# Two transformer blocks on one core: a re-ordered instruction schedule, and fused high-weight matmuls of 512 columns in both feed-forward blocks

## The chip, the core and the metric

The kernel runs on one core of a Trainium2 chip. The metric is device time in microseconds, from the first to the last instruction of one execution plus the launch and end around it. The engines named below are TensorE (PE in the profile; its weight loads are PEld), VectorE (DVE), ScalarE (ACT), GpSimd (POOL) and SyncE (SP), which issues the transfers.

## The reference

Input `x` has 256 tokens of 1024 features, float32. The reference is two blocks in a row, cut here to what matters:

```python
# block 1
h = rms_norm(x); proj = h @ w_in                 # 8 projections
o_sb  = stick_breaking_attention(sb_q, sb_k, sb_v)     # 8 heads of 64
log_a = log_sigmoid(g_low @ w_gate_up + b) / 16
o_gla = silu(g_out) * rms_norm(gated_linear_attention(g_q, g_k, g_v, log_a))  # 4 heads
x = x + (sigmoid(gate_sb) * (o_sb @ w_proj_sb) + sigmoid(gate_gla) * (o_gla @ w_proj_gla)) @ w_out
x = rms_norm(x + square(relu(rms_norm(x) @ w_ff1)) @ w_ff2)            # 4096 hidden
# block 2
q, k, v, ... = rms_norm(x) @ w_in_2
kc, vc = gelu(blocks(k_c) @ w1) @ w2             # compressed keys and values
nsa  = sum over compressed, selected, window attention (8 heads, 2 groups), gated
conv = silu(layer_norm(depthwise_conv_31(a * sigmoid(ag))))
mem  = cross attention to 256 memory tokens
h = x + merge(nsa, conv, mem) @ w_out_2
out = h + (silu(hn @ w_gate) * (hn @ w_up)) @ w_down                    # 2816 hidden
```

## The kernel before, in words

**Precision.** Every large product is made from float32 data split in two parts for TensorE's fp32r input: hi is the value rounded to fp32r, lo the rest. `mm3` issues three matmuls into one accumulator: hi·hi, hi·lo, lo·hi (L562 to L564).

**Weight chunks.** All weights stream through a ring of three slots (`RING = 3`) as 143 chunks of 1 MB (128 partitions x 2048). SyncE loads chunk n into `raw` when the lo part of chunk n-3 is made; ScalarE casts it to `whi` (`split_hi`, L1115) once TensorE is done with chunk n-3; VectorE makes `wlo = raw - whi` (`split_lo`, L1638); TensorE takes the chunk when `wlo` is there. The order of the chunks is the list at the top of the kernel, and each engine's program is written out in that order, with each chunk's evacuation and side work at fixed places in it. Each engine runs its own program strictly in order.

**Chunk kinds.** A 256-wide projection chunk is 48 matmuls of 256 columns. A contraction chunk (`into_residual`) is 24 matmuls of 512 columns. A compression chunk (`wk0, wk1, wv0, wv1`, function `compress`) is 16 matmuls of 256 columns. Results of projections alternate between two PSUM banks; a bank must be evacuated (`drained`) before the next but one chunk uses it (`free_unit`).

**Block 1.** Chunk 0 is `low`. From chunk 9 on, stick-breaking attention (n = 9 to 18) and gated linear attention (GLA) run between the chunks. GLA has 8 units u, one every second chunk (n = 9 + 2u): `gla_sums` (two float32 matmuls of 512 columns, L714), ScalarE's exponential (L1240), GpSimd's factors (`gla_factors`: 14 products at L505 and one at L508 or L510), then one chunk later `gla_scores` (L722) and VectorE's mask and reduction (`gla_mask`, L1749 to L1756). `gla_values` follows every fourth chunk from n = 13. The chunks 19 to 26 are sigmoid gates, whose evacuation on ScalarE is Abs, Exp, Ln, then the cast of chunk n+3, then Exp.

**Feed-forward 1** is 16 pairs: `expand` (one `w_ff1` chunk, hidden features on partitions, both 128-feature halves in one PSUM bank) and `contract` (one `w_ff2` chunk). The order on TensorE is expand f+1, contract f. ScalarE relu (L1333) and square (L1335), VectorE square (L1848) and lo part (L1851). **Feed-forward 2** is 11 triples gate f+1, up f+1, down f; ScalarE takes tanh of the gate (L1596), VectorE multiplies.

**Between blocks** ("seams"), `block_norm` on VectorE and ScalarE normalises the residual, TensorE transposes it (`turn_normed`, L657), and ScalarE and VectorE make `hT_hi` (L1165) and `hT_lo` (L1708) before the next chunk can start. Event numbers: 0 before chunk `low`, 2 before feed-forward 1, 3 before block 2, 4 before feed-forward 2.

**Block 2.** s counts chunks from `kcvc`. The order before is kcvc, ca0, cg0, wk0, wk1, kk, q0, wv0, wv1, q1, vv, ca1, cg1, qm0, qm1, then gates. Key and query norms are seven "head sums" on TensorE (L883), fed by ScalarE squares (L1414). `hidden_turn` and small matmuls make compressed keys. VectorE computes 124 convolution taps (L1989) spread over s = 3 to 25 by `taps_by`. Attention units start at s = 8: scores at s, ScalarE exponentials (L1462) in the same s, transposes at s+2, values at s+3.

Of the kernel before, what the change touches and what calls it, by code (L numbers as in the profile page):

```python
# [13 lines left out]
P = 128  # L14
# [17 lines left out]
def two_block_kernel(  # L32
# [90 lines left out]
    ATT = [(k, a, g) for a in range(TT) for g in range(2) for k in "swc"] + [("m", a, 0) for a in range(TT)]  # L123
    ATT_AT = 8

    with ExitStack() as ctx:
# [17 lines left out]
        hT_hi = sb("hT_hi", [P, KT, T], F32R)  # L144
        hT_lo = sb("hT_lo", [P, KT, T], F32R)
# [38 lines left out]
        a_ls = xn[:, 0, :].rearrange("p (a n) -> p a n", a=TT)  # L184
# [9 lines left out]
        decay_sum = TMP[:, 0:1152].rearrange("p (l t) -> p l t", t=P)  # L194
        mask = TMP[:, 1152:2176].rearrange("p (l t) -> p l t", t=P)
# [7 lines left out]
        ACC_FLAT = [PS[:, 2 * a:2 * a + 2, :].rearrange("p b n -> p (b n)") for a in range(TT)]  # L203
        S_gla = TMP[:, 4352:4736].rearrange("p (i t) -> p i t", t=P)
# [45 lines left out]
        def gate_tile(name):  # L250
# [13 lines left out]
        hi_made, lo_made, chunk_used = sem("hi_made"), sem("lo_made"), sem("chunk_used")  # L264
        drained = [sem("drained0"), sem("drained1")]
# [14 lines left out]
        h1_relu, h1_sq, h1_hi, h1_lo = (sem(n) for n in ("h1_relu", "h1_sq", "h1_hi", "h1_lo"))  # L280
# [16 lines left out]
        taps, cv_mean, cv_mid, cv_sq, cv_var, cv_ln, cv_root, cv_exp, cv_y, cv_lin, cv_sig, cv_f, cv_hi, cv_lo = (  # L297
            sem(n) for n in ("taps", "cv_mean", "cv_mid", "cv_sq", "cv_var", "cv_ln", "cv_root", "cv_exp", "cv_y", "cv_lin",
# [132 lines left out]
        def _(pool):  # L431
# [30 lines left out]
            keep(decay_sum[:, 8, :], [[1, P]], 0, -1)  # L462

# [27 lines left out]
            def gla_factors(u):  # L491
# [8 lines left out]
                for l in range(LEVELS):  # L500
                    hf = 1 << l
                    e = E[:, l + 1 - a, :].rearrange("p (b s x) -> p b s x", s=2, x=hf)
                    d = QK[:, l, :].rearrange("p (b s x) -> p b s x", s=2, x=hf)
                    for s, m in ((0, k), (1, q)):
                        pool.tensor_tensor(d[:, :, s, :], e[:, :, s, :],  # L505
                                           m.rearrange("p (b s x) -> p b s x", s=2, x=hf)[:, :, s, :], ALU.mult)
# [1652 lines left out]
```

## Time and profile before

| | us |
|---|---|
| median of 3 runs | 997.95 |
| range of the runs | 995.75 to 1002.14 |
| the profiled execution, own time | 995.86 |
| its span, first to last instruction | 994.1 |

| engine | busy us | share of span |
|---|---|---|
| TensorE matmul | 952.6 | 96% |
| TensorE weight load | 873.4 | 88% |
| VectorE | 585.2 | 59% |
| ScalarE | 517.5 | 52% |
| GpSimd | 85.9 | 9% |

Mean granted TensorE clock of the span: 0.986. The transfers moved 155.37 MB, 156 GB/s on average. A matmul's row in the profile lasts longer than the distance to the next row, because matmuls are pipelined: 0.28 us for 256 columns where the next one starts 0.12 us later. So for TensorE the distance between starts counts, not the duration. The clock column PEclk is the share of full speed (2.4 GHz) that was granted; 0.5 is the other level, 1.2 GHz.

### The profile page before, as it was taken

The numbers are of one execution on the slowest core, as the hardware profiler recorded it, in microseconds if no ns is written. First come the engines' busy times: TensorE is split into PE (matmuls) and PEld (weight loads), VectorE is DVE, ScalarE is ACT, GpSimd is POOL, SyncE is SP. The second block draws the span as 40 slices with busy tenths as digits, with TensorE's granted clock in tenths as the row PEclk, the third lists the DMA queues.
The fourth block names the chain that finished last, engine by engine and source line by source line (L and its number), as shares of the span: only waits on it lengthen the run. The fifth ranks groups of instructions, "written<-read, shape, count | busy, mean of one in ns | idle before, by whom it ended". The sixth has DMA issues, their size and how long they took to land.

```text
span 994.1 us, 16151 instructions
## 1 busy us (share of the span) xinstructions
PE 952.6 (96%) x6700; PEld 873.4 (88%) x6700; DVE 585.2 (59%) x704; ACT 517.5 (52%) x738; POOL 85.9 (9%) x220
## 2 busy tenths in 40 slices
PE   7999999898999999999987889999999989999998
PEld 7998888888988999999887888888999879999997
DVE  5334455655766554554575996655685655555554
ACT  6445545465446444444367667776646453434332
POOL 8202332233010000000010000000000000000000
PEclk9899999999999999999999889999999999999999
DMA  8464332427555565555643554334334545555551
GB/s 265 149 198 133 108 105 85 129 92 238 170 172 170 173 197 184 208 169 176 204 151 104 170 169 128 107 107 128 128 128 170 169 127 176 197 177 183 196 170 43
DMA packets 121817, 155.37 MB, mean 156 GB/s; under 512 B 2649, under 2 KB 107201, under 8 KB 121762
## 3 DMA queue, kind: packets, MB, share of 16 engines
q1 hardware_dynamic: 120848, 151.57, 47.5%
q0 software_dynamic: 864, 2.98, 0.9%
q8 instruction: 40, 0.66, 0.3%
q14 instruction: 15, 0.12, 0.0%
q10 hardware_dynamic: 50, 0.04, 0.0%
HBM read 153.53 MB, written 1.05 MB: 155 GB/s over the span
## 4 chain that ended last, share of the span: by engine, by line
PE 84%; DVE 7%; ACT 5%; POOL 2%; issue 1%; DMA 0%; SPq 0%; ACTq 0%; DVEq 0%
PE PS L562 24%; PE PS L563 24%; PE PS L564 24%; DVE wlo L1638 3%; ACT whi L1115 2%; PE PS L722 1%; POOL TMP L505 1%; PE PS L974 1%; DVE AR L1989 1%; PE PS L944 1%; PE PS L714 1%; PE PS L925 1%; PE PS L681 1%; PE PS L670 1%; DMA res<-in_x_dram 0%
## 5 line engine op out<-in xcount | busy, mean ns | idle before, releaser
L1638 DVE TENSOR_TENSOR wlo<-raw,whi 128x2048 fp32r<-128x2048 f32 (+1 forms) x143 | 326.5, 2284 | 236.6 <-ACT whi L1115 236.5
L562 PE MATMUL PS<-hT_hi,whi 128*128 128x256 f32 x1224 | 353.3, 289 | 7.2 <-DVE hT_lo L1708 4.1
L563 PE MATMUL PS<-hT_lo,whi 128*128 128x256 f32 x1224 | 350.3, 286 | 0.0
L564 PE MATMUL PS<-hT_hi,wlo 128*128 128x256 f32 x1224 | 350.3, 286 | 0.0
L1115 ACT CAST whi<-raw 128x2048 fp32r<-128x2048 f32 (+1 forms) x143 | 270.6, 1893 | 117.8 <-PE PS L564 117.6
L562 PEld LDWEIGHTS PS<-hT_hi,whi 128*128 128x128 f32 x1224 | 239.2, 195 | 9.7 <-issue 4.5
L563 PEld LDWEIGHTS PS<-hT_lo,whi 128*128 128x128 f32 x1224 | 238.9, 195 | 1.0
L564 PEld LDWEIGHTS PS<-hT_hi,wlo 128*128 128x128 f32 x1224 | 238.8, 195 | 0.0
L562 PE MATMUL PS<-whi,aT_hi 128*128 128x512 f32 x216 | 84.3, 391 | 0.0
L563 PE MATMUL PS<-wlo,aT_hi 128*128 128x512 f32 x216 | 84.3, 390 | 0.0
L564 PE MATMUL PS<-whi,aT_lo 128*128 128x512 f32 x216 | 84.0, 389 | 0.0
L562 PE MATMUL PS<-whi,hT_hi 128*128 128x256 f32 (+1 forms) x240 | 76.5, 319 | 0.0
L563 PE MATMUL PS<-wlo,hT_hi 128*128 128x256 f32 (+1 forms) x240 | 74.7, 311 | 0.0
L564 PE MATMUL PS<-whi,hT_lo 128*128 128x256 f32 (+1 forms) x240 | 74.7, 311 | 0.0
L562 PE MATMUL PS<-oT_hi,whi 128*128 128x256 f32 x224 | 64.2, 287 | 5.3 <-ACT xn L1204 1.5
L563 PE MATMUL PS<-oT_lo,whi 128*128 128x256 f32 x224 | 63.4, 283 | 0.0
L564 PE MATMUL PS<-oT_hi,wlo 128*128 128x256 f32 x224 | 63.4, 283 | 0.0
L1989 DVE SCALAR_TENSOR_TENSOR AR<-AR,cw 128x256 f32<-128x256 f32 x120 | 49.4, 479 | 0.2
L562 PEld LDWEIGHTS PS<-oT_hi,whi 128*128 128x128 f32 x224 | 42.9, 192 | 6.5 <-issue 3.8
L563 PEld LDWEIGHTS PS<-wlo,hT_hi 128*128 128x128 f32 x240 | 45.7, 191 | 2.9 <-issue 0.5
L562 PEld LDWEIGHTS PS<-whi,hT_hi 128*128 128x128 f32 x240 | 45.7, 191 | 2.9 <-issue 0.5
L564 PEld LDWEIGHTS PS<-whi,aT_lo 128*128 128x128 f32 x216 | 40.6, 188 | 8.6
(336 smaller groups left out, 1145.5 us busy)
## 6 DMA issues: line engine op xcount, KB each, us to landing
raw<-in_w_in_dram SPq DMA_DIRECT2D x47, 1024.0 KB, 5.2
raw<-in_w_ff_dram SPq DMA_DIRECT2D x32, 1024.0 KB, 5.2
raw<-in_w_gate_dram SPq DMA_DIRECT2D x11, 1024.0 KB, 5.3
raw<-in_w_up_dram SPq DMA_DIRECT2D x11, 1024.0 KB, 5.3
raw<-in_w_down_dram SPq DMA_DIRECT2D x11, 1024.0 KB, 5.0
raw<-in_w_out_dram SPq DMA_DIRECT2D x8, 1024.0 KB, 4.9
raw<-in_w_proj_gla_dram SPq DMA_DIRECT2D x4, 1024.0 KB, 5.1
raw<-in_w_mem_kv_dram SPq DMA_DIRECT2D x4, 1024.0 KB, 5.1
```

The costliest lines, as they stand in the source:

```text
L505: pool.tensor_tensor(d[:, :, s, :], e[:, :, s, :], m.rearrange("p (b s x) -> p b s x", s=2, x=hf)[:, :, s, :], ALU.mult)
L562: pe.matmul(dst, a_hi, b_hi, start=start, stop=False, skip_group_check=True)
L563: pe.matmul(dst, a_hi, b_lo, start=False, stop=False, skip_group_check=True)
L564: return pe.matmul(dst, a_lo, b_hi, start=False, stop=stop, skip_group_check=True)
L670: pe.matmul(z[:, 0:256], kT_sb[r, h // 2, 0:P], qT_sb[r, h // 2, :], start=True, stop=False, skip_group_check=True)
L681: pe.matmul(z[:, 0:384], negtri[:, :], spv, start=False, stop=False, skip_group_check=True)
L714: mm = pe.matmul(PS[:, 6 + c, :], a_ls[:, a, h * P:(h + 1) * P], decay_sum[:, a + 4 * c:a + 4 * c + 4, :], start=True, stop=True)
L722: pe.matmul(PS[:, 6 + l // 4, (l % 4) * P:(l % 4) * P + P], QK[:, l, :], QK[:, l, :], start=True, stop=True)
L925: pe.matmul(PS[:, h % 2, h // 2 * L:(h // 2 + 1) * L], q, k, start=h < 2, stop=False, skip_group_check=True)
L1115: act.copy(whi[:, n % RING, 0:width], raw[:, n % RING, 0:width]).then_inc(hi_made, 1)
L1638: dve.tensor_tensor(wlo[:, n % RING, 0:width], raw[:, n % RING, 0:width], whi[:, n % RING, 0:width].bitcast(F32), ALU.subtract).then_inc(l ...
L1989: ins = dve.scalar_tensor_tensor(cacc[:, f, :], src, cw[:, f, k:k + 1], cacc[:, f, :], ALU.mult, ALU.add)
```

## The change

1. **Chunk order of block 2**: compression chunks alternate with full ones. Head sums, `hidden_turn` and the norms move with them; the two memory-key norms come later (e = 4, 5 instead of 0, 1), attention units of the first token tile run s, w, s, w, c, c. `taps_by` has 14 taps done by the end of s = 9 (43 before).
2. **GLA**: `gla_sums` uses fp32r: log decays split in hi and lo (`a_hi`, `a_lo`), the 0/1 matrix as `decay_r`: four fp32r matmuls in place of two float32 ones. For u = 5, 6, 7 ScalarE's exponential moves ahead of the cast, and VectorE makes three of the seven levels of factors.
3. **Start**: chunk `low` is used at 66 columns, chunk 1 is cast and split in two halves, and TensorE starts on the first.
4. **Seams**: the last quarter of transposes (`turn_last`) moves behind the first two k of the first chunk (events 2 and 4); a split is cut in half around the root of event 3; at event 4 one `split_lo` moves from ahead of `block_norm` to behind the turned tiles, and a table load moves behind them too.
5. **Feed-forward**: `hT_hi` and `hT_lo` become one tile `hT`, and `wide` replaces `expand` and `gate_or_up`: the high weights stream both parts in one 512-column matmul, the low weights the high part in one of 256. Each half of 128 features fills a bank; ScalarE copies the lo half out, VectorE adds the hi half. Feed-forward 1's loop is 2 x 6 steps and 3 written out (5 x 3 before).
6. A `cg` chunk's bank is freed by VectorE's minimum instead of by the product after the exponential.

```diff
+    key_chunk("kk", 0)
     compress_chunk(0, 0)
+    chunk("q0", cols(w_in_2, 0))
     compress_chunk(0, 1)
-    key_chunk("kk", 0)
-    chunk("q0", cols(w_in_2, 0))
+    key_chunk("vv", 1)
     compress_chunk(1, 0)
+    chunk("q1", cols(w_in_2, CW))
     compress_chunk(1, 1)
-    chunk("q1", cols(w_in_2, CW))
-    key_chunk("vv", 1)
...
-        FN_AT = [2, 4, 6, 7, 8, 10, 15]
+        FN_AT = [4, 6, 10, 11, 12, 14, 15]
...
-                return 62 * max(s - 2, 0) // 10 if s <= 12 else min(62 + 62 * (s - 12) // 13, 124)
+                return 2 * max(s - 2, 0) if s <= 9 else min(14 + 110 * (s - 9) // 16, 124)
...
                 for c in range(2):
-                    mm = pe.matmul(PS[:, 6 + c, :], a_ls[:, a, h * P:(h + 1) * P],
-                                   decay_sum[:, a + 4 * c:a + 4 * c + 4, :], start=True, stop=True)
+                    d = decay_r[:, a + 4 * c:a + 4 * c + 4, :]
+                    pe.matmul(PS[:, 6 + c, :], a_hi[a][:, h * P:(h + 1) * P], d, start=True, stop=False)
+                    mm = pe.matmul(PS[:, 6 + c, :], a_lo[a][:, h * P:(h + 1) * P], d, start=False, stop=True)
...
             for n in range(at["projs0"]):
                 name = list(at)[n]
                 evac(name)
+                if n in (19, 21, 23):
+                    gla_exp((n - 9) // 2)
                 split_hi(n + RING)
...
+                if n in (19, 21, 23):
+                    dve.wait_ge(gf_exp, (n - 9) // 2 + 1)
+                    for l in range(LOW_LEVELS, LEVELS):
+                        ins = gla_factor(dve, (n - 9) // 2, l)
+                    ins.then_inc(gf_up, 1)
...
+            def wide(n, bank, it=0, event=None):
                 take(n, it)
                 w_hi, w_lo = parts(n, CW)
                 for c in range(2):
                     for k in range(KT):
                         if c == 0:
+                            if event is not None and k == 2:
+                                turn_last(event)
                             turned(event, k)
-                        mm = mm3(PS[:, 4 + j, c * T:(c + 1) * T], w_hi[:, k, c * P:(c + 1) * P],
-                                 w_lo[:, k, c * P:(c + 1) * P], hT_hi[:, k, :], hT_lo[:, k, :], k == 0, k == KT - 1)
+                        f = slice(c * P, (c + 1) * P)
+                        pe.matmul(PS[:, bank + c, :], w_hi[:, k, f], hT[:, k, :, :].rearrange("p w t -> p (w t)"),
+                                  start=k == 0, stop=False, skip_group_check=True)
+                        mm = pe.matmul(PS[:, bank + c, 0:T], w_lo[:, k, f], hT_hi[:, k, :], start=False, stop=k == KT - 1,
+                                       skip_group_check=True)
...
             def relu_square(f, it=0):
...
+                act.copy(relu[:, j, :].rearrange("p (c t) -> p c t", c=2), two_banks(4 + 2 * (f % 2))[1]).then_inc(h1_b, 1)
+                act.wait_ge(h1_sq, f + 1 + 3 * it)
+                act.copy(aT_hi[:, j].rearrange("p a t -> p (a t)"), sq[:, j, :]).then_inc(h1_hi, 1)
...
+                dve.wait_ge(h1_b, f + 1 + 3 * it)
+                dve.tensor_tensor(s, two_banks(4 + 2 * (f % 2))[0], s, ALU.add).then_inc(h1_sum, 1)
+                dve.wait_ge(h1_sum, f + 1 + 3 * it)
+                dve.scalar_tensor_tensor(sq[:, j, :], relu[:, j, :], 0.0, relu[:, j, :], ALU.max, ALU.mult).then_inc(h1_sq, 1)
...
+                pe.wait_ge(s_gate, f + 1 + 2 * it)
+                wide(FFN2 + 2 + 3 * f, 4, it)
+                pe.wait_ge(s_up, f + 1 + 2 * it)
+                wide(FFN2 + 3 + 3 * f, 6, it)
                 down(FFN2 + 4 + 3 * f, f, j, it)
...
             block_norm(3, res, x3_of)
-            split_lo(after_ffn1 + 2)
+            split_lo_half(after_ffn1 + 2, 0)
             token_root(5)
             normed(5, [res[:, a, :] for a in range(TT)], [xn[:, a, :] for a in range(TT)], width=512)
+            split_lo_half(after_ffn1 + 2, 1)
...
-            for c in range(3):
+            for c in range(2):
                 split_lo(FFN2 - 1 + c)
             block_norm(4, xn, scaled_in_place(4))
             turned_lo(4, hT_hi, hT_lo, G_FFN)
+            split_lo(FFN2 + 1)
             split_lo(FFN2 + 2)
```

## Rows read from the trace of the kernel before

**Rows 1.** The page, parts 1, 4 and 5: busy, the chain's engines, the taps
```profile
PE 952.6 (96%) x6700; PEld 873.4 (88%) x6700; DVE 585.2 (59%) x704; ACT 517.5 (52%) x738; POOL 85.9 (9%) x220
...
PE 84%; DVE 7%; ACT 5%; POOL 2%; issue 1%; DMA 0%; SPq 0%; ACTq 0%; DVEq 0%
...
L1989 DVE SCALAR_TENSOR_TENSOR AR<-AR,cw 128x256 f32<-128x256 f32 x120 | 49.4, 479 | 0.2
```

**Rows 2.** A stretch: length; PE, PEld, DVE, ACT, POOL busy; clock; DMA; GB/s
```profile
514.00:593.00 79.00, 67.20 (x492) 63.35 (x493) 62.18 (x115) 49.13 (x89) 0.00 (x0) 0.89 0.53 160
```

**Rows 3.** Timeline, TensorE, feed-forward 1: start, duration, engine, line, instruction
```profile
399.93 0.39 PE L563 MATMUL PS<-wlo,aT_hi 128*128 128x512 f32 x1
...
402.20 0.39 PE L564 MATMUL PS<-whi,aT_lo 128*128 128x512 f32 x1
...
402.42 0.28 PE L562 MATMUL PS<-hT_hi,whi 128*128 128x256 f32 x1
...
407.10 0.28 PE L562 MATMUL PS<-hT_hi,whi 128*128 128x256 f32 x1
```

**Rows 4.** One line (L1333): durations in ns, first and last start
```profile
L1333 ACT ACTIVATE relu<-PS x16: 597/598/598, 324.1 to 486.9; 128x512 f32<-128x512 f32 x16
```

**Rows 5.** The same of L1596, the tanh of feed-forward 2
```profile
L1596 ACT ACTIVATE relu<-PS x11: 597/598/598, 815.7 to 980.1; 128x512 f32<-128x512 f32 x11
```

**Rows 6.** Groups, 345 to 485 us: busy us, mean ns, idle before
```profile
L1638 DVE TENSOR_TENSOR wlo<-raw,whi 128x2048 fp32r<-128x2048 f32 x26 | 59.6, 2292 | 39.7 <-ACT whi L1115 39.7
...
L1115 ACT CAST whi<-raw 128x2048 fp32r<-128x2048 f32 x25 | 47.6, 1902 | 31.2 <-PE PS L564 31.2
```

**Rows 7.** Timeline, TensorE: the sums of GLA unit 3, and the next
```profile
141.07 1.98 PE L714 MATMUL PS<-TMP,xn 128*128 128x512 f32 x4
142.89 0.27 PE L747 MATMUL PS<-ident,AR 128*128 128x128 f32 x1
```

**Rows 8.** Waits of TensorE: us in total, times, longest
```profile
PE PS L722 <- POOL TMP L510: 5.1, 2, 2.6
...
PE PS L722 <- POOL TMP L508: 1.7, 1, 1.7
```

**Rows 9.** Timeline, ScalarE: the exponential of GLA unit 5
```profile
183.23 1.00 ACT L1240 ACTIVATE TMP<-PS 128x1024 f32<-128x1024 f32 x1
```

**Rows 10.** Timeline, GpSimd: the factors of unit 5
```profile
184.31 4.73 POOL L505 TENSOR_TENSOR TMP<-TMP,AR 128x64 f32<-128x64 f32 x14 [14.93 <-ACT TMP L1240]
```

**Rows 11.** Timeline, VectorE: the reduction of unit 7
```profile
231.01 1.99 DVE L1756 TENSOR_REDUCE TMP<-TMP 128x128 f32<-128x1024 f32 x1
```

**Rows 12.** Timeline, TensorE: the values that need it
```profile
234.10 0.60 PE L739 MATMUL PS<-AR,TMP 128*128 128x256 f32 x2
```

**Rows 13.** Timeline, GpSimd and TensorE: unit 0's last factor and its scores
```profile
87.01 0.46 POOL L508 TENSOR_TENSOR TMP<-TMP,AR 128x128 f32<-128x128 f32 x1
...
87.53 1.71 PE L722 MATMUL PS<-TMP 128*128 128x128 f32 x13
```

**Rows 14.** Timeline, TensorE: start of chunk 1
```profile
18.32 0.38 PE L562 MATMUL PS<-hT_hi,whi 128*128 128x256 f32 x1 [2.01 <-DVE wlo L1638]
```

**Rows 15.** Timeline, TensorE, block 2: where it waited, chunks 2 to 11
```profile
538.48 0.30 PE L856 MATMUL PS<-whi,aT_hi 128*66 128x256 f32 x1 [1.76 <-DVE aT_hi L2045]
...
545.08 1.13 PE L883 MATMUL PS<-xn,negone 128*128 128x512 f32 x2 [2.66 <-ACT xn L1414]
547.31 0.55 PE L562 MATMUL PS<-hT_hi,whi 128*128 128x256 f32 x1 [1.11 <-DVE AR L1878]
...
573.17 0.63 PE L883 MATMUL PS<-TMP,negtri 128*128 128x30 f32 x2 [4.88 <-ACT TMP L1414]
```

**Rows 16.** Timeline, VectorE and ScalarE, seam before feed-forward 2
```profile
791.89 2.29 DVE L1638 TENSOR_TENSOR wlo<-raw,whi 128x2048 fp32r<-128x2048 f32 x1 [3.15 <-ACT whi L1115]
...
800.42 1.28 ACT L1095 ACT_TABLE_LOAD   x1
```

**Rows 17.** Timeline, TensorE: transposes at the same seam
```profile
803.51 0.66 PE L657 MATMUL PS<-ident,xn 128*128 128x128 f32 x4 [2.42 <-DVE hT_lo L1708]
```

More of the change, by code:

```diff
@@ L499, in gla_factors @@
                 q, k = gqT[:, h, tok], gkT[:, h, tok]
[L500 to L506, printed above, removed]
+                for l in range(LOW_LEVELS if u in LATE_UNITS else LEVELS):
+                    gla_factor(pool, u, l)
                 if a == 0:
@@ L583, in feature_major @@
                 n, u = at[name], unit_of[name]
-                take(n)
+                if n == 1:
+                    pe.wait_ge(lo_half, 1)
+                else:
+                    take(n)
                 w_hi, w_lo = parts(n, width)
+                m = LOW if name == "low" else P
                 for f in range(width // P):
@@ L646, in turn_normed @@
                         pe.wait_ge(xn_made, done)
-                    for q in range(4 if a else first):
+                    for q in range(4 if event in (0, 3) else 3):
                         if a == 1 and q == 2:
@@ L827, in _, with step1 @@
                 pe.wait_ge(drained[b], (units_before_ffn1 - b + 1) // 2)
-            expand(FFN1, 0, event=2)
-            with pe.Fori(0, (F1 - 1) // 3) as it:
-                for j in range(3):
-                    expand(FFN1 + 1 + 2 * j, (j + 1) % 3, it)
-                    contract(FFN1 + 2 + 2 * j, j, j, it)
+            wide(FFN1, 4, event=2)
+            def step1(f, it=0):
+                wide(FFN1 + 1 + 2 * f, 4 + 2 * ((f + 1) % 2), it)
+                contract(FFN1 + 2 + 2 * f, f, f % 3, it)
+            with pe.Fori(0, 2) as it:
+                for f in range(6):
+                    step1(f, 2 * it)
+            for f in range(12, F1 - 1):
+                step1(f)
             contract(after_ffn1 - 1, F1 - 1, 0, last=True)
@@ L1058, in _ @@
                 pe.wait_ge(drained[b], (units - b + 1) // 2)
-            def gate_or_up(n, bank, it=0, event=None):
-                take(n, it)
-                w_hi, w_lo = parts(n, CW)
-                for c in range(2):
-                    for k in range(KT):
-                        if c == 0:
-                            turned(event, k)
-                        mm = mm3(PS[:, bank, c * T:(c + 1) * T], w_hi[:, k, c * P:(c + 1) * P],
-                                 w_lo[:, k, c * P:(c + 1) * P], hT_hi[:, k, :], hT_lo[:, k, :], k == 0, k == KT - 1)
-                mm.then_inc(chunk_used, 1)
             def down(n, f, j, it=0, last=False):
@@ L1313, in _ @@
                     turned_hi(1, oT_hi, G_MEM)
-            junk_hT = [w[:, 0:4, :].rearrange("p f t -> p (f t)") for w in (hT_hi, hT_lo)]
+            junk_hT = [hT[:, 2 * i:2 * i + 2, :, :].rearrange("p f w t -> p (f w t)") for i in range(2)]
             block_norm(2, xn, junk_hT)
```

388 lines of the change are left out of this document (228 added, 160 removed).

## The prediction, made before the changed kernel ran

> **What bounds the kernel now.** I read the page's busy times and its chain first: TensorE is busy 96% of the span and holds 84% of the chain [rows 1]. Then the stretches: in the first eleven chunks of block 2 it is busy 67.2 of 79 us at clock 0.89 [rows 2]. Then the waits of TensorE and the timelines around them [rows 8, 14, 15, 17]. So there are two kinds of stretch. In the loops only fewer or shorter matmuls help. In the GLA part, the start of block 2 and the seams TensorE waits for VectorE, ScalarE or GpSimd, and there the order counts.
>
> What one matmul costs is read from start-to-start distances. From 399.93 to 402.20 lie 10 matmuls of 512 columns: 0.227 us each. From 402.42 to 407.10 lie 39 of 256 columns: 0.120 us each [rows 3]. At 2.4 GHz the columns alone take 0.213 and 0.107, so each instruction carries about 13 ns that do not grow with its columns. The feed-forward loops run at exactly this pace: the reads of the 16 expands span 162.8 us [rows 4], and one expand (48 x 0.120 = 5.8) plus 14 pairs (5.76 + 24 x 0.227 = 11.2) make 162.7. In feed-forward 2, 9 triples of 2 x 5.76 + 5.45 = 17.0 and one of 11.5 make 164.2, against 164.4 measured [rows 5]. No wait hides in either loop.
>
> **Part by part.**
>
> *Fused matmuls.* Three matmuls of 256 (0.360 us) become one of 512 and one of 256 (0.347): 13 ns less per group. There are 16 groups in a chunk and 16 + 22 = 38 chunks, so 608 groups: **7.9 us**. Columns streamed do not change, 12288 per chunk. The Trainium skill ("TensorE: Matmul & The Clock Gate", section "Wait — 56ns, not 53.3ns?") gives a fixed cost of about 2.5 ns per warm matmul. By it the fusion would be worth 608 x 2.5 ns = 1.5 us, an estimate from that page; the two distances of rows 3 disagree with it. Bounds of the term from rows: 0 (if the 13 ns go with every 256 columns, which the 0.227 speaks against) to 7.9.
>
> The new passes are hidden. In feed-forward 1 ScalarE now waits, between its two reads, for VectorE's add and square, and the casts of two chunks are queued behind it. From the end of an expand: copy 0.6, two VectorE passes of 512 elements (a 2048-element pass takes 2.29, so 0.6 to 0.7 each), ScalarE 0.6, cast 1.9, VectorE's split 2.3 [rows 4, 6]: 6.8, about 7 with handovers. TensorE needs that chunk after one contract and one expand, 5.45 + 5.55 = 11.0 us. Slack 4 us. In feed-forward 2 the gate and up banks are single, but each is refilled only 11 us after it was filled, and its copy and add come first in the queues: also hidden. Cost 0.
>
> *GLA sums.* Two float32 matmuls take 1.82 us [rows 7]; four fp32r ones would take 4 x 0.227 = 0.91. Eight units: 7.3. At unit 0, GpSimd ends at 87.47 and TensorE arrives at 87.53 [rows 13]: nothing is left there, and GpSimd's start follows the attention mask, not the sums. So 0.7 comes back as a wait. **6.6 us**. The gate's extra copy and subtraction lie in the first 35 us, where both engines wait for TensorE.
>
> *GLA units 5 to 7.* TensorE waits 5.1 + 1.7 = 6.8 us for GpSimd [rows 8]. ScalarE's exponential starts at 183.23 [rows 9] after a cast (1.9) and a gate exponential (0.6); moved ahead of both it starts about 2.3 earlier. GpSimd's 14 products take 4.73 [rows 10]; it keeps 8, which is 2.0 less. Together 4.3, more than any single wait (2.6), so all three go, and VectorE's six small products run beside. What is late next: VectorE's reduction of unit 7 ends at 233.00 [rows 11], and the values that need it started at 234.10 [rows 12], slack 1.1. The reduction is behind chunk 24's split, whose timing is set by the end of chunk 24, while TensorE now arrives 2.6 earlier: 1.5 comes back. Net **5.3 us**. Ends: 3 (the same at unit 5) and 6.8.
>
> *Start.* Chunk 1 waits 2.01 us for its split [rows 14]. With halves, cast and split before the first matmul shrink by half of 1.9 and 2.3, 2.1 us; VectorE is also held by the turned tiles, so **1.7 us**; ends 0 and 2.0. The 66-column `low` shortens work that nobody waits for: 0.
>
> *Block 2's order.* The four waits are 1.8, 2.7, 1.1 and 4.9: 10.4 us [rows 15]. They come where two compression chunks follow each other: TensorE is through one in 16 x 0.120 = 1.9 us, ScalarE and VectorE need 1.9 + 2.3 per chunk plus norms and taps. In the new order a full chunk (5.8 us) lies between them; VectorE has 29 fewer taps by the end of s = 9 (120 of them take 49.4 us [rows 1], so about 12 us less; these come back at s = 10 to 25, beside chunks of 5.8 us and more); and the `cg0` bank is freed before the split instead of behind it. Laying the queues out with these durations leaves waits of 0.5 us before the head sum of kk, 1.8 before that of q0 (ScalarE copies the keys twice first) and 0.8 and 1.2 before the second and third attention scores: 4.3. Gain 6.1. The clock 0.89 over 79 us is 8.7 us of full-speed time [rows 2]; about 1.5 of it fell into waits. I keep one stretch at 1.2 GHz behind the seam and one later, 3.4 in all: gain 3.8. The two memory-key norms arrive in chunks 12 to 14, where ScalarE is the tightest; laid out, 1 us. **9 us**; ends 3 (waits only move) and 15.
>
> *Seams.* Event 3: half a split (1.15) leaves ScalarE's and VectorE's path: 0.9. Event 4: the split at 791.89 holds VectorE until 794.18, and the first token tile of the last contraction is complete half a chunk (2.7 us) before TensorE ends it, so VectorE could have begun earlier; of the 2.3 us I take 1.4 (ends 0 and 2.3); the 1.28 us table load stands ahead of the turned tiles [rows 16], for which TensorE waits 2.4 [rows 17]: 1.3. `turn_last` makes the last quarter late by about 0.4 at events 2 and 4. **2.8 us**; ends 0.5 and 4.
>
> **Sum.** 7.9 + 6.6 + 5.3 + 1.7 + 9 + 2.8 = 33.3. The profiled execution's own time was 995.9, so 962.6. It lies 2.1 us under the median of the runs, 997.95, so the median after should be near **965**.
>
> **The rivals.**
> 1. *The waits of block 2 only change place* (chance 0.20). For it: ScalarE is the queue behind most of them, and its work per chunk stays. Against: VectorE, 62.2 of 79 us busy [rows 2], loses 12 us. Then 3 instead of 9, the clock low as before, and unit 5 adds a wait: 965 + 6 + 2 = 973.
> 2. *The fusion gives nothing* (0.05), the 13 ns being tied to data, not to instructions: 965 + 7.9 = 973. The page "TensorE: Matmul & The Clock Gate" of the Trainium skill, section as above, points towards this case.
> 3. *Block 2 stays at 2.4 GHz* throughout and its waits shrink further (0.12): 6 us more, 959.
> 4. *Slower than before* (0.02): the round trip ScalarE, VectorE, ScalarE ahead of the casts of feed-forward 1 becomes its bound. It decides once it exceeds 11.0 us from the expand's end; to eat 33 us and another 10 over 15 pairs it must be 2.9 us above, 14 us in place of 7. Nothing in rows 6 is near that: VectorE is idle 39.7 us of that stretch.
> 5. My forecast: 0.61, own range 958 to 972.
>
> **How the numbers follow.** Range 955 to 979: down to rival 3 with the start and seams at their good ends, up to rivals 1 and 2 with half of the lower bounds at once. One per cent is 10 us, about what a measurement of this kernel tells from no change. Slower by over 1% is rival 4 and unnamed mishaps, 0.02. Within 1% needs the terms at nearly all their lower ends (0 + 6.6 + 3 + 0 + 3 + 0.5 = 13), 0.05. Faster by over 1%: 0.93.
>
> **What would show it.** Right: in feed-forward 1 the reads of the 16 expands span 159.6 us (15 x 0.21 less), 512 and 256 columns at 0.227 and 0.120; no wait of the scores of units 5 to 7 for GpSimd, and one of about 1.5 us of unit 7's values for VectorE; TensorE's waits between chunks 2 and 11 of block 2 near 4; no table load between the seam's norm and its turned tiles. Wrong: a distance of 0.24 or more behind the fused matmul; TensorE waiting for `wlo` inside a loop; clock under 0.9 in the first chunks of block 2.

## The result, and the profile after

| | before | after |
|---|---|---|
| median of the runs | 997.03 us (4 runs) | 966.38 us (4 runs, 965.28 to 967.08) |
| profiled execution, own time | 995.9 | 966.8 |
| its span, mean granted clock | 994.1, 0.986 | 965.1, 0.993 |

The ratio is 0.9682, with a 95% interval of 0.9646 to 0.9719: 3.2% faster. The forecast was 965.

The page after, parts 1 and 4 [rows 1]: busy time, share and instructions of each engine, then the chain's engines:

```profile
PE 938.4 (97%) x6092; PEld 835.4 (87%) x6092; DVE 616.1 (64%) x764; ACT 529.0 (55%) x763; POOL 86.1 (9%) x203
...
PE 85%; ACT 6%; DVE 6%; issue 2%; POOL 1%; DMA 1%; SPq 0%; ACTq 0%; DVEq 0%; POOLq 0%
```

TensorE issues 608 matmuls fewer and bounds the kernel as before; VectorE has 31 us more work, and TensorE's only new waits for it are 0.5 us (L776) and 0.4 us (L1088). TensorE's waits in the list of waits (us in total, times, longest), where rows 8, 14, 15 and 17 stood:

```profile
PE PS L858 <- DVE hT L1774: 3.9, 4, 1.5
PE PS L585 <- DVE hT L1774: 3.2, 2, 1.8
PE PS L970 <- ACT TMP L1508: 2.0, 2, 1.1
...
PE PS L759 <- POOL TMP L533: 1.6, 2, 0.8
...
PE PS L938 <- ACT xn L1469: 1.5, 1, 1.5
...
PE PS L776 <- DVE TMP L1825: 0.5, 1, 0.5
PE PS L989 <- ACT TMP L1517: 0.4, 1, 0.4
...
PE PS L585 <- DVE wlo L1854: 0.2, 1, 0.2
```

**Where the 29.1 us between the two profiled executions went.** Set the two timelines side by side at the same event. The lead is how much earlier "after" reaches it; a minus sign marks a stage in which it lost time:

| up to | event, start before and after | lead | of it in this stage | forecast |
|---|---|---|---|---|
| sums of GLA unit 0 | 78.06, 74.73 | 3.3 | start 3.3 | 1.7 |
| values of unit 7 | 234.10, 220.71 | 13.4 | sums 5.5, units 5 to 7 4.6 | 6.6 and 5.3 |
| first read of feed-forward 1 | 324.08, 311.48 | 12.6 | seam -0.9, fusion 0.1 | -0.4 |
| last read of it | 486.9, 472.6 | 14.3 | fusion 1.7 | (7.9 in all) |
| first chunk of block 2 | 514.23, 499.10 | 15.1 | seam 0.8 | 0.9 |
| sums of the convolution | 733.10, 707.73 | 25.4 | block 2 10.2 | 9 |
| bank of `up` 0 read | 815.7, 788.6 | 27.1 | seam 1.6, fusion 0.2 | 2.3 |
| last of them | 980.1, 951.0 | 29.1 | fusion 1.9 | |

Every stage has the sign that was forecast; the fusion brought 3.9 in place of 7.9, the start twice its term.

**The clock.** Stretches (length, busy times, granted clock, DMA share, GB/s) around each stretch of TensorE at 1.2 GHz, first before, then after:

```profile
26.00:36.00 10.00, 10.00 (x48) 8.35 (x47) 3.58 (x3) 4.37 (x8) 6.42 (x18) 0.66 0.64 202
514.00:520.00 6.00, 5.77 (x35) 5.80 (x36) 4.64 (x8) 2.16 (x2) 0.00 (x0) 0.72 0.57 179
546.00:554.00 8.00, 6.89 (x35) 6.72 (x35) 7.93 (x13) 5.25 (x9) 0.00 (x0) 0.57 0.80 254
570.00:578.00 8.00, 4.83 (x28) 4.54 (x29) 7.90 (x19) 5.67 (x11) 0.00 (x0) 0.57 0.55 159
594.00:598.00 4.00, 4.00 (x23) 4.00 (x22) 3.64 (x6) 3.61 (x14) 0.00 (x0) 0.57 0.01 2
```

```profile
26.00:30.00 4.00, 4.00 (x21) 3.95 (x21) 2.59 (x3) 2.77 (x6) 3.73 (x5) 0.57 0.93 270
500.00:505.00 5.00, 5.00 (x31) 4.99 (x30) 3.59 (x5) 1.50 (x1) 0.00 (x0) 0.66 0.59 190
562.00:566.00 4.00, 4.00 (x24) 3.77 (x25) 3.20 (x10) 3.97 (x11) 0.00 (x0) 0.57 0.82 262
608.00:614.00 6.00, 6.00 (x31) 3.81 (x31) 3.10 (x13) 4.93 (x8) 0.00 (x0) 0.72 0.58 175
```

Length times (1 - clock), summed: 13.7 us lost before, 6.8 after. That is 6.9 of the 29.1, 1.7 of it at the start.

In each of the 14 profiles the loss is a multiple of 1.7 us, and the number of stretches differs from run to run of one kernel; that makes most of its scatter. So two numbers are given for each experiment below: its median, and the mean over its runs of span times granted clock ("full-speed time"), in which the stretches are left out. For the four runs of the changed kernel the second lies within 0.6 us of its mean; the third decimal of the clock alone is worth 0.5 us either way in one run. It has a weakness: a wait inside a stretch at 1.2 GHz is counted by half. The last column of the table below is the mean of span times (1 - clock). Before: 980.7 (15.3 us lost to the clock, 9 runs beside e1 to e4). After: 958.3 (6.3 lost). So of the 30.7 us between the medians 22.4 is less work and fewer waits, and some 8 to 9 is clock.

### The profile page after: what moved, and what is told of

The parts are those of the page before. It is cut to its first block, busy times and chain, and to the rows that moved or that the text cites. A ratio compares the mean times of both kernels' runs of the same rounds, so it can differ in the third digit from the quotient of the medians.

```text
span 965.1 us, 14962 instructions
## 1 busy us (share of the span) xinstructions
PE 938.4 (97%) x6092; PEld 835.4 (87%) x6092; DVE 616.1 (64%) x764; ACT 529.0 (55%) x763; POOL 86.1 (9%) x203
## 3 DMA queue, kind: packets, MB, share of 16 engines
HBM read 153.53 MB, written 1.05 MB: 160 GB/s over the span
## 4 chain that ended last, share of the span: by engine, by line
PE 85%; ACT 6%; DVE 6%; issue 2%; POOL 1%; DMA 1%; SPq 0%; ACTq 0%; DVEq 0%; POOLq 0%
PE PS L585 17%; PE PS L587 17%; PE PS L586 17%; PE PS L858 15%; PE PS L860 7%; ACT whi L1151 3%; DVE wlo L1695 2%; PE PS L759 1%; PE PS L1019 1%; PE PS L989 1%; PE PS L970 1%; POOL TMP L217 1%; DVE hT L1774 1%; PE PS L715 1%; DMA res<-in_x_dram 1%
## 5 line engine op out<-in xcount | busy, mean ns | idle before, releaser
L1695 DVE TENSOR_TENSOR wlo<-raw,whi 128x2048 fp32r<-128x2048 f32 x140 | 320.8, 2292 | 164.2 <-ACT whi L1151 163.9
L1151 ACT CAST whi<-raw 128x2048 fp32r<-128x2048 f32 x141 | 268.5, 1904 | 91.9 <-PE PS L587 91.8
L858 PE MATMUL PS<-hT,whi 128*128 128x512 f32 x608 | 216.4, 399 | 3.9 <-DVE hT L1774 3.9
L585 PE MATMUL PS<-hT,whi 128*128 128x256 f32 (+1 forms) x616 | 178.9, 290 | 3.4 <-DVE hT L1774 3.2
L586 PE MATMUL PS<-hT,whi 128*128 128x256 f32 (+1 forms) x616 | 175.9, 286 | 0.0
L587 PE MATMUL PS<-hT,wlo 128*128 128x256 f32 (+1 forms) x616 | 175.8, 285 | 0.0
L860 PE MATMUL PS<-hT,wlo 128*128 128x256 f32 x608 | 170.7, 281 | 0.0
L585 PEld LDWEIGHTS PS<-hT,whi 128*128 128x128 f32 (+1 forms) x616 | 119.7, 194 | 4.9 <-issue 3.6
L586 PEld LDWEIGHTS PS<-hT,whi 128*128 128x128 f32 (+1 forms) x616 | 119.6, 194 | 0.2
L587 PEld LDWEIGHTS PS<-hT,wlo 128*128 128x128 f32 (+1 forms) x616 | 119.3, 194 | 0.0
L860 PEld LDWEIGHTS PS<-hT,wlo 128*128 128x128 f32 x608 | 114.8, 189 | 0.9
L585 PE MATMUL PS<-whi,hT 128*128 128x256 f32 (+1 forms) x240 | 75.7, 316 | 0.0
L587 PE MATMUL PS<-whi,hT 128*128 128x256 f32 (+1 forms) x240 | 74.7, 311 | 0.0
```

Of the source, the lines that this page charges most:

```text
L585: pe.matmul(dst, a_hi, b_hi, start=start, stop=False, skip_group_check=True)
L586: pe.matmul(dst, a_hi, b_lo, start=False, stop=False, skip_group_check=True)
L587: return pe.matmul(dst, a_lo, b_hi, start=False, stop=stop, skip_group_check=True)
L858: pe.matmul(PS[:, bank + c, :], w_hi[:, k, f], hT[:, k, :, :].rearrange("p w t -> p (w t)"), start=k == 0, stop=False, skip_group_check=True)
L860: mm = pe.matmul(PS[:, bank + c, 0:T], w_lo[:, k, f], hT_hi[:, k, :], start=False, stop=k == KT - 1, skip_group_check=True)
L1151: act.copy(whi[:, n % RING, :], raw[:, n % RING, :]).then_inc(hi_made, 1)
```

## Experiments

Each is an edit of the changed kernel. The ratios are to the kernel before, on the same chip. e1 to e4, e5 to e8 and e9 to e12 ran on three chips, beside the kernel before (medians 997.43, 999.00 and 998.77; full-speed times 980.7, 981.0 and 980.7) but not beside the changed kernel. The intervals of all ratios but those of e8 and e9 overlap with that of after, so what is said below of differences of 1 to 5 us rests on the full-speed time and the traces. Single runs of e6 and e11 spread over 2 to 3 us in full-speed time, those of e9 over 1.4, of the others over 1.1 at most.

| | median | ratio (95%) | full-speed time | lost to the clock |
|---|---|---|---|---|
| after | 966.38 | 0.9682 (0.9646 to 0.9719) | 958.3 | 6.3 |
| e1 three matmuls of 256 | 969.54 | 0.9716 (0.9694 to 0.9738) | 962.5 | 5.4 |
| e2 low ones behind | 962.56 | 0.9656 (0.9635 to 0.9677) | 955.9 | 5.6 |
| e3 quarter turned ahead | 964.17 | 0.9666 (0.9644 to 0.9689) | 957.2 | 5.4 |
| e4 six products on GpSimd | 966.43 | 0.9685 (0.966 to 0.971) | 957.9 | 6.6 |
| e5 and reductions ahead | 964.16 | 0.9653 (0.9628 to 0.9677) | 955.5 | 7.1 |
| e6 old taps | 970.56 | 0.9721 (0.9692 to 0.9751) | 960.5 | 8.7 |
| e7 warm at the seam | 967.54 | 0.9685 (0.966 to 0.971) | 958.5 | 7.5 |
| e8 units 5 to 7 as before | 978.22 | 0.9794 (0.9769 to 0.982) | 964.8 | 11.7 |
| e9 e2, e3 and e5 together | 958.58 | 0.9584 (0.9559 to 0.9609) | 950.8 | 5.6 |
| e10 start not halved | 971.44 | 0.9727 (0.9704 to 0.975) | 960.7 | 8.7 |
| e11 seam 4 as before | 970.76 | 0.9719 (0.9694 to 0.9745) | 958.8 | 10.3 |
| e12 float32 sums | 971.42 | 0.9722 (0.9699 to 0.9746) | 963.1 | 5.8 |

### What the fusion is worth: e1 and e2

The timeline of TensorE in feed-forward 1, after: the start and the end of a wide chunk's 16 groups (start, duration, engine, line, instruction).

```profile
400.14 0.39 PE L858 MATMUL PS<-hT,whi 128*128 128x512 f32 x1
400.36 0.28 PE L860 MATMUL PS<-hT,wlo 128*128 128x256 f32 x1
400.48 0.40 PE L858 MATMUL PS<-hT,whi 128*128 128x512 f32 x1
400.71 0.28 PE L860 MATMUL PS<-hT,wlo 128*128 128x256 f32 x1
400.83 0.40 PE L858 MATMUL PS<-hT,whi 128*128 128x512 f32 x1
...
405.78 0.40 PE L585 MATMUL PS<-whi,aT_hi 128*128 128x512 f32 x1
```

5.64 us for 16 groups is 0.3525 each, between the 0.360 of three matmuls of 256 and the 0.347 of the forecast [rows 3].

e1:
```
-  pe.matmul(PS[:, bank + c, :], w_hi[:, k, f], hT[:, k, :, :], start=k == 0)
+  pe.matmul(PS[:, bank + c, 0:T], w_hi[:, k, f], hT_hi[:, k, :], start=k == 0)
+  pe.matmul(PS[:, bank + c, T:2 * T], w_hi[:, k, f], hT_lo[:, k, :])
```

> The changed kernel, but both feed-forward blocks stream the high and the low part of x in two matmuls of 256 columns again, in the same banks and the same order; ScalarE's and VectorE's passes stay as changed. In the changed kernel 16 groups of 512 + 256 columns run from 400.14 to 405.78, 0.3525 us a group, where the forecast had 0.347 and three matmuls of 256 took 0.360. Forecast's theory (13 ns a group saved): 608 x 13 ns = 7.9 us slower than the changed kernel, 974.3. Theory from the trace of after (7 ns a group): 4.3 us slower, 970.6. Third (the fusion is worth nothing, the loops only read so): 966.4. The rounds of this group tell these apart; the 16 reads of the expands should span 162.8 us again in the second case, and their distance stays 11.1 in the third.

Measured: 969.54, full-speed time 4.2 longer than after. The reads of the 16 expands (duration in ns, first and last start), e1 and then after [rows 4]:

```profile
L1374 ACT COPY relu<-PS x16: 587/587/587, 312.2 to 475.1; 128x512 f32<-128x512 f32 x16
```

```profile
L1372 ACT COPY relu<-PS x16: 587/588/588, 311.5 to 472.6; 128x512 f32<-128x512 f32 x16
```

162.9 us and 161.1. The fusion as it stands is worth 4.2, 7 ns a group: the second theory. The loops keep TensorE's pace in both, so the new passes are hidden, as the forecast had it.

e2:
```
   for k in range(KT):
       pe.matmul(PS[:, bank + c, :], w_hi[:, k, f], hT[:, k, :, :], ...)
-      mm = pe.matmul(PS[:, bank + c, 0:T], w_lo[:, k, f], hT_hi[:, k, :], ...)
+  for k in range(KT):
+      mm = pe.matmul(PS[:, bank + c, 0:T], w_lo[:, k, f], hT_hi[:, k, :], ...)
```

> The changed kernel, but in every feed-forward chunk except the two that stand at a seam the eight matmuls of 512 columns of a half run first and the eight of 256 columns behind them, where the changed kernel alternates them. Theory A (the 5.7 ns that a group costs more than 0.347 fall at each change of width): of 16 changes from 512 to 256 in a chunk 2 are left, so 36 chunks x 14 x 5.7 ns = 2.9 us faster than the changed kernel, 963.5; a chunk takes 5.56 in place of 5.64 us. Theory B (they belong to the 512 columns of x itself, whichever matmul stands beside them): no change, 966.4, and the matmuls of 512 columns stand 0.232 apart in a row of eight.

Measured: 962.56, full-speed time 2.4 shorter than after. Its timeline:

```profile
399.71 1.98 PE L858 MATMUL PS<-hT,whi 128*128 128x512 f32 x8
401.53 1.11 PE L865 MATMUL PS<-hT,wlo 128*128 128x256 f32 x8
402.48 2.00 PE L858 MATMUL PS<-hT,whi 128*128 128x512 f32 x8
```

Half a chunk takes 402.48 - 399.71 = 2.77 us, 0.346 for each pair: the forecast's 0.347. Same matmuls, same operands, other order. So theory A holds: a step from 512 to 256 columns costs 5 to 6 ns (in after the next start comes 0.2325 behind a wide matmul, in a row of eight 0.2275; behind a narrow one it is 0.12 in both). Alternating at every step had cost 2.4 of the 6.6 us that the fusion brings with both edits.

### The GLA part: e12, e8, e4, e5

e12 (sums; VectorE also copies the log decays in place of splitting them):
```
-  pe.matmul(PS[:, 6 + c, :], a_hi[a][...], d, start=True, stop=False)
-  mm = pe.matmul(PS[:, 6 + c, :], a_lo[a][...], d, start=False, stop=True)
+  mm = pe.matmul(PS[:, 6 + c, :], a_ls[...], decay_sum[...], start=True, stop=True)
```

> The changed kernel with the GLA sums as two float32 matmuls a unit again, in place of four of fp32r. Forecast's term: 6.6 us slower, 973.0. By the traces (a unit's sums take 1.82 in place of 1.05 us, 136.20 to 137.25; eight units, less the 0.63 us wait of unit 0 that goes): 5.5 slower, 971.9. Rival (TensorE, now later by 0.77 in each unit, finds the products of units 5 and 7 ready, so that their waits of 0.8 go too): 3.9 slower, 970.3. The waits of the scores for GpSimd in its trace tell the last two apart.

Measured: 971.42, full-speed time 4.8 longer. Its waits of TensorE have no row for L533 any more, and that of unit 7's values is longer:

```profile
PE PS L776 <- DVE TMP L1825: 1.3, 1, 1.3
```

So: 8 x 0.77 = 6.2, less the GpSimd waits that it hides (0.6 + 1.6), plus 0.8: 4.8. The sums are worth 4.8 here, not 6.6; and the waits that the trace of after shows for units 5 and 7 are the sums' own gain given back.

e8 (units 5 to 7): `LATE_UNITS = ()`, the exponentials back behind cast and gate exponential, no products on VectorE.

> The changed kernel with the GLA units 5 to 7 as before: ScalarE's exponential behind cast and gate exponential, all 14 products on GpSimd. Forecast's theory: net 5.3 us slower than the changed kernel, 971.7. By the traces (a unit costs 2.54 in place of 0.78 less than before, 3 x 1.76, less the 0.67 lost as unit 7's values wait): 4.6 slower, 971.0, and waits of 2.6, 1.7 and 2.5 us of the scores of units 5 to 7 for GpSimd. Rival (the waits had gone anyway since the sums are shorter): under 2 us slower.

Measured: 978.22, 11.8 slower, more than twice any theory. Its waits:

```profile
PE PS L759 <- POOL TMP L533: 6.7, 2, 3.4
...
PE PS L759 <- POOL TMP L531: 3.1, 2, 2.5
```

9.8 us in all, 0.6 of it at unit 0 as in after; so 9.2 at units 5 to 7, where the kernel before had 6.8 [rows 8]: with the sums 0.77 shorter TensorE arrives earlier at each unit, and each wait grows by about as much. Full-speed time is 6.5 longer. The other 5.4 is the clock: behind each of the three waits stands a stretch at 1.2 GHz that neither kernel has there.

```profile
180.00:184.00 4.00, 0.70 (x3) 0.71 (x4) 0.96 (x2) 3.94 (x5) 3.24 (x12) 0.91 0.83 261
184.00:186.00 2.00, 2.00 (x11) 2.00 (x11) 2.00 (x1) 0.23 (x1) 0.00 (x0) 0.50 0.00 0
...
224.00:228.00 4.00, 4.00 (x23) 4.00 (x22) 3.31 (x3) 0.18 (x1) 0.08 (x1) 0.57 0.72 260
```

So my two GLA terms do not add as I added them: without the moved exponentials the sums' gain at these three units, 2.4 of the 5.5 us, turns into waiting.

Why do units 5 and 7 still wait 0.8? In the trace of after, GpSimd's eight products of unit 7, the seventh of them, and VectorE beside them:

```profile
207.23 4.50 POOL L217 TENSOR_TENSOR TMP<-TMP,AR 128x64 f32<-128x64 f32 x8 [10.80 <-ACT TMP L1272]
...
209.07 2.38 POOL L217 TENSOR_TENSOR TMP<-TMP,AR 128x64 f32<-128x64 f32 x1
...
208.98 2.29 DVE L1695 TENSOR_TENSOR wlo<-raw,whi 128x2048 fp32r<-128x2048 f32 x1
```

One product that takes 0.29 in unit 4 (14 in 4.08 us) takes 2.38 here, from 209.07 to 211.45; the split ends at 211.27. GpSimd stood still while VectorE split. The Trainium skill ("SBUF — State Buffer", section "Who interferes with whom") says that a VectorE instruction with two operands in SBUF contends with a GpSimd instruction that reads SBUF, over ports that one of them holds exclusively; the row agrees. I had read 4.73 for 14 products [rows 10] and taken 6/14 of it off; those 4.73 hold such a hold-up as well (the first product took 1.02, until VectorE's split had ended), and the eight run into one just the same.

e4: `LATE_UNITS, LOW_LEVELS = (5, 6, 7), 3`

> The changed kernel, but GpSimd keeps 6 of the 14 level products of GLA units 5 to 7 and VectorE takes 8. In the trace of after, 8 products take GpSimd 4.50 us (207.23 to 211.73), the last ones starting at 209.07 and ending after VectorE's split (208.98 to 211.27); in unit 4, without VectorE beside them, 14 take 4.08. Theory A (VectorE's split, which reads two operands, holds GpSimd up until it ends): six products are through in 6 x 0.33 = 2.0 us, ahead of the split, the two waits of 0.8 us for GpSimd go, up to 0.8 comes back as unit 7's values wait for VectorE: 0.8 to 1.6 us faster than the changed kernel, 965.2. Theory B (each product is slow beside any work of VectorE, 0.56 us): six take 3.4 us and still run beside the split; the waits go as well, so the time is the same and the six products' length tells them apart. Theory C (the waits only move to unit 7's values): 966.4.

Measured: 966.43. Its six products on the timeline, then, from its list of waits, those of the values:

```profile
206.92 1.90 POOL L217 TENSOR_TENSOR TMP<-TMP,AR 128x64 f32<-128x64 f32 x6 [14.16 <-ACT TMP L1272]
```

```profile
PE PS L776 <- DVE TMP L1825: 2.2, 2, 1.5
```

Theory A is right on the product (0.32 each ahead of the split, 2.6 us less than for eight), theory C on the time: the 1.6 us of waits came back whole one link later, as waits for VectorE's reduction, which stands behind a split.

e5 (on top of e4; the calls behind the split go for these units):
```
+  if n in (20, 22, 24):
+      gla_mask((n - 10) // 2)
   split_lo(n + RING)
```

> The kernel of e4 (six products on GpSimd, eight on VectorE), and for GLA units 5 to 7 VectorE masks the scores and reduces them ahead of that chunk's split, not behind it. In e4 the six products took 1.90 us and ended 2.5 us earlier than the eight, but TensorE then waited 2.2 us for the reductions of units 5 and 7, which stand behind a split (214.84 to 217.13 for unit 7). Theory A (the reduction behind the split is the next link): those waits go, 2 us or a little more than e4, 964.3. Theory B (the split that is now 3.4 us later is missed by TensorE): as much comes back as a wait for wlo. Theory C (the link is the scores themselves, not VectorE): 966.4.

Measured: 964.16, full-speed time 2.4 shorter than e4 and 2.8 than after; no wait for L1825 is left and none for `wlo` has come. Theory A.

### Block 2: e6 and e7

e6: `taps_by` as in the kernel before.

> The changed kernel with the old spread of the convolution's taps in the new chunk order: 29 taps more by s = 9, 12 us more of VectorE there, and as many fewer at s = 10 to 25. It parts the two things that the block 2 term holds. Theory A (VectorE's load in the first eleven chunks was what counted): waits for VectorE and half-speed stretches come back there, 3 to 5 us slower than the changed kernel, 970. Theory B (the order of the chunks alone did it): 966 to 967, TensorE's waits between chunks 2 and 11 stay at 3.8 us.

Measured: 970.56, full-speed time 2.2 longer and 2.4 us more lost to the clock. The two rows of the waits that moved:

```profile
PE PS L970 <- ACT TMP L1508: 3.9, 2, 2.8
...
PE PS L938 <- ACT xn L1469: 3.0, 1, 3.0
```

1.9 and 1.5 more than in after. Theory A has the time; but both rows name ScalarE, where it expected waits for VectorE. So of the 10.2 us in block 2 about 4 belong to the later taps. The rest is put down to the order of the chunks with its norms and the earlier free bank of `cg` only because nothing else is left: no run undid the order by itself, since the banks and the waits are written for it.

e7: `keep_warm(7, 9)` behind `turn_normed(3)`.

> The changed kernel, but TensorE fills its 1.80 us wait at the start of block 2 with nine matmuls of 128 columns of the identity into an unused bank (0.19 us each, 1.7 us). In the changed kernel the granted clock is 1.00 in 495 to 500 and 0.58 in 500 to 504, which costs 1.7 us. Theory A (the idle time ahead of it is what lowers the clock there): the stretch at half speed is gone and the kernel is 1.7 us faster, 964.7. Theory B (the transposes and weight loads of the 15 us ahead, or something else, lower it): no change, 966.4, or up to 0.3 slower from the added matmuls.

Measured: 967.54, full-speed time 958.5: no gain. The stretch at half speed behind the seam was gone in its profile, but one stood at 540 that after had not, and the start's was twice as long:

```profile
501.00:505.00 4.00, 4.00 (x34) 3.98 (x33) 3.77 (x7) 2.38 (x3) 0.00 (x0) 1.00 0.97 301
540.00:546.00 6.00, 6.00 (x40) 6.00 (x40) 5.30 (x9) 2.99 (x5) 0.00 (x0) 0.72 0.77 244
```

The profiles of e3, e4 and e5 show the same exchange without the added matmuls. So this experiment doesn't say what lowers the clock at the seam: where the stretches fall differs between executions, and one warmed place doesn't change their number.

### Start and seams: e10, e11, e3

e10:
```
-  act.copy(whi[:, 1, 0:1024], raw[:, 1, 0:1024]).then_inc(hi_half, 1)
-  act.copy(whi[:, 1, 1024:2048], raw[:, 1, 1024:2048]).then_inc(hi_made, 1)
+  act.copy(whi[:, 1, :], raw[:, 1, :]).then_inc(hi_made, 1)
```
(and the split and TensorE's wait alike)

> The changed kernel, but chunk 1 is cast and split whole at the start, not in halves. Forecast's term: 1.7 us slower, 968.1, and TensorE waits 1.9 to 2.0 us for that split in place of 0.21. Rival (the first stretch at half speed, 6.8 us before and 3.4 after, hangs on that wait): another 1.7 us, 969.8. Second rival (halves cost as much in fixed time as they bring): 966.4.

Measured: 971.44, 5.1 slower: 2.4 in full-speed time and 2.5 of clock. The wait is 3.0 in its profile, where the kernel before had 2.0 [rows 14]. The difference is the split itself, 3.26 us in place of 2.29: GpSimd's cast of the 0/1 matrix, new with the fp32r sums, started 0.03 us ahead of it and took 1.14. TensorE's wait, then GpSimd and VectorE on the timeline:

```profile
PE PS L585 <- DVE wlo L1689: 3.0, 1, 3.0
...
16.21 1.14 POOL L490 CAST aT_hi<-TMP 128x1152 fp32r<-128x1152 f32 x1
...
16.24 3.26 DVE L1689 TENSOR_TENSOR wlo<-raw,whi 128x2048 fp32r<-128x2048 f32 x1 [0.67 <-ACT whi L1299]
```

Two stretches behind it are at half speed:

```profile
19.00:23.00 4.00, 3.45 (x16) 3.45 (x17) 4.00 (x3) 1.00 (x1) 3.75 (x5) 0.59 0.57 166
29.90:36.90 7.00, 7.00 (x29) 5.66 (x28) 4.50 (x5) 4.46 (x9) 2.53 (x3) 0.51 0.50 158
```

The first rival fits in size, but that the length of the stretch goes with the wait is not shown: the profiles of e7 and e9 have one of 6.8 us at 25 to 33 as well, without the wait. Shown is that the mean loss to the clock is 2.5 larger over five runs. The term at the start was the wait (chunk 1 starts 1.85 earlier by the traces); the 1.7 of clock on top was not in the sum.

e11: third split ahead of `block_norm(4)`, `tables(EXP_TANH)` ahead of `turned_hi(4)`.

> The changed kernel, but at the seam ahead of feed-forward 2 the third split stands ahead of the norm and the load of ScalarE's table ahead of the turned tiles, as before. Forecast's terms: 1.4 + 1.3 = 2.7 us slower, 969.1. From the traces: TensorE turns its first tiles 1.35 us earlier against the end of block 2 than before, and ScalarE's first read of them is 1.0 us nearer to that: 2.4 slower, 968.8. Rival (the table load is hidden behind the wait for the last quarter): 1.4, 967.8.

Measured: 970.76, 4.4 slower. Counted from the first warm-up matmul of the seam, the first wide matmul starts 779.02 - 770.52 = 8.5 us later in e11, 775.86 - 769.77 = 6.1 in after: 2.4 us, of which the split is 1.4 (first turned tile 3.9 against 2.6) and the table load 1.0. Forecast 2.7. On top stands once more a stretch at half speed that after does not have, 8 x 0.43 = 3.4 us. Full-speed time is only 0.5 longer and the loss to the clock 4.0: part of the waits lies inside the stretch, where they count by half, so this run does not part waiting from clock. Timeline and stretch of e11:

```profile
770.52 2.17 PE L657 MATMUL PS<-ident 128*128 128x128 f32 x18
...
774.46 0.87 PE L682 MATMUL PS<-ident,xn 128*128 128x128 f32 x6 [1.78 <-DVE xn L1767]
...
779.02 0.76 PE L858 MATMUL PS<-hT,whi 128*128 128x512 f32 x1 [1.84 <-DVE hT L1774]
```

```profile
774.90:782.90 8.00, 5.86 (x26) 4.86 (x24) 3.58 (x10) 5.68 (x11) 0.00 (x0) 0.57 0.00 0
```

The kernel before has waits of that length there [rows 17] and clock 1.00 in its profile, so such a wait brings the stretch in some executions and not in others.

e3: `if event is not None and k == 0: turn_last(event)`, in place of `k == 2`.

> The changed kernel, but the last quarter of x is turned ahead of the first feed-forward matmul of each block, not behind its second group. In the trace of after, TensorE's waits at both seams are 1.50 (first matmul) and 0.43 us (last quarter), and from the first wait's end to ScalarE's read of the bank it takes 7.08 where the kernel before took 6.47 with the tiles ahead. Theory A (the last quarter is on the path because it is turned too late): the 0.43 us wait goes and 0.6 to 0.8 us a seam come back, 1.2 to 1.6 in all, 965.0. Theory B (the quarter only changes place, and what counts is when VectorE has the first low part): 0 to 0.3 us, 966.3.

Measured: 964.17, full-speed time 1.1 shorter. From the first turned tile to ScalarE's first read it takes 309.3 - 300.0 = 9.3 us at seam 2, as in the kernel before (324.1 - 314.8 = 9.3), and 311.5 - 301.5 = 10.0 in after; at seam 4 it is 9.8 against 10.6. Theory A: `turn_last` behind the second group costs 0.7 a seam, where the forecast had 0.4.

### All three: e9

> The changed kernel with the three edits that gained by themselves: the matmuls of 512 columns of a half first and those of 256 behind them (e2), the last quarter of x turned ahead of the first feed-forward matmul (e3), six products on GpSimd with the reductions ahead of the splits (e5). Span times mean clock, which leaves the half-speed stretches out, was 958.3 for the changed kernel, 955.9, 957.2 and 955.5 for these. If the three gains stand in different stages and add: 958.3 - 2.4 - 1.1 - 2.8 = 952.0, and with 6 us for the clock and 1.7 around the span 959.7. If the earlier turned quarter only helps where the first chunk alternates widths, or half-speed stretches take the gains back: 961.5 or more.

Measured: 958.58, 0.9584 (0.9559 to 0.9609): 7.8 us faster than the changed kernel and the fastest of all. Full-speed time 950.8, 7.5 shorter, against 6.3 if the three gains add; where the other 1.2 comes from stays open.

## Why the prediction was right, point by point

The median came out 1.4 us from the forecast. Every step had the right sign; the largest miss, the fusion, was off by a factor of two. The sum was 33.3 against 29.1 between the profiled executions, so that the profiled one was forecast 4.2 too low. What closed the gap is luck: I added 2.1 us as the distance from profile to median, while the profile after lies 0.4 above its median; the runs of before simply lost more to the clock than the profiled one (0.986; the others 0.979 to 0.988, over half of them 0.983 or 0.984). Luck too is that too much for the fusion, the sums, the units and the seams met too little for the start and block 2, where 6.8 us of clock came in and 3.8 were forecast.

- **Fused matmuls** (7.9): 4.2. The 13 ns are per instruction, not tied to data, and e2 brings it to 6.6; the step that failed is taking 0.227 and 0.120 from rows in which each width followed its own kind. So the 16 reads span 161.1 us, not the 159.6 that the forecast named as its sign. The rival "the fusion gives nothing" fell. The Trainium skill ("TensorE: Matmul & The Clock Gate", section "Wait — 56ns, not 53.3ns?") gives about 2.5 ns a matmul, which made 1.5 us in all; these traces show 7 ns saved a group alternating and 13 in rows. The hidden passes were right: no read in the loops waits beyond TensorE's pace.
- **GLA sums** (6.6): 5.5 by the traces, 4.8 by e12. Four matmuls with their entry take 1.05, not 0.91; the 0.7 given back at unit 0 was right (0.63).
- **Units 5 to 7** (5.3): 4.6. "Together 4.3 ... so all three go" failed for units 5 and 7, which still wait 0.8 each: 8 of 14 products take 4.50, not 2.7, since VectorE's split stops GpSimd. That TensorE arrives 0.77 earlier at each unit was missing too. Unit 7's values wait 0.5, not 1.5, because TensorE had already waited 0.8 for its scores; e4 shows the 1.5.
- **Start** (1.7): the wait fell by 1.8; the clock gave 1.7 more in this pair of profiles. The 66 columns give nothing, as forecast, though not for the reason given: they don't shorten `low`, whose last matmul starts at 16.03 before and 15.98 after.
- **Block 2** (9): 10.2. Waits laid out by hand: 0.5, 1.8, 0.8 and 1.2; measured none, 1.5, 0.9 and 1.1, and 0.4 before a turn. Clock: 3.8 forecast, 10.3 less 5.1 by the rows above, partly inside waits that went as well. Neither "the waits only change place" nor "stays at 2.4 GHz" happened.
- **Seams** (2.8): 0.8 - 0.9 + 1.6 = 1.5. Event 3 was right (0.9). At event 4 split and table are 2.4 in place of 2.7. The mis-sized term is `turn_last`, 0.7 twice.
- **Slower** by the round trip in feed-forward 1: nothing near it; from the second on the 16 reads are evenly 11.1 us apart.

## What to carry to other kernels

Fusing matmuls that share their weights saves the fixed part of each instruction only if equal widths then follow each other: run the wide ones of a group first and the narrow ones behind. Terms along one chain do not add: a cut on TensorE comes back as a wait at the next product of GpSimd or reduction of VectorE, so lay out what arrives earlier after each cut, and ask which VectorE instruction with two SBUF operands stands beside a GpSimd one. Where the clock drops behind waits, compare kernels by span times granted clock as well; in this kernel waits of 2 to 3 us cost 1.6 to 1.8 times their length (e8, e10 and e11: 7.6, 2.8 and 2.4 us of waiting cost 11.8, 5.1 and 4.4).

## What the hardware showed that was not expected

- A change from a matmul of 512 to one of 256 columns costs 5 to 6 ns over either in its own row.
- GpSimd's product of 0.3 us took 2.38 while VectorE ran one subtraction of two SBUF operands; in e10 such a subtraction, 2.29 otherwise, took 3.26 behind a GpSimd cast of 1.14 that had started just ahead of it.
- Stretches at 1.2 GHz come in lengths of 3.4 and 6.8 us; their number differs between runs of one kernel. Behind the waits of 1.8 to 3.4 us restored in e8, e10 and e11 the profile has one each time, and the loss to the clock grew by 2.4 to 5.4 us there. Why one place has it in one execution and another in the next stays open.
